# Scattering expert outputs by rank with plain writes, and finishing the last expert's slots on their own, in a mixture-of-experts decoder step

## What is computed

```python
# h = rmsnorm(x, ln_moe_g); 320 tokens, 4 groups of 8 experts, top-1 group, top-2 experts in it
hid = silu(xblk @ w_gate[e]) * (xblk @ w_up[e])          # per expert: (2048 x 512) twice
yb  = hid @ w_down[e]                                      # per expert: (512 x 2048)
y   = zeros(N + 1, D).at[slot_tok].add(yb * slot_w[:, None])
x   = x + y[:N]                                            # residual
out = rmsnorm(x, final_norm_g)                             # y_prompt (256 rows), y_sample (64 rows)
```

## Time and profile before

| | us |
|---|---|
| Median of 3 runs (1901.27 to 1910.1) | 1905.28 |
| The profiled execution's own time | 1904.04 |
| Its span, first to last instruction | 1902.2 |

### The profile page before, as it was taken

How to read it: one execution, slowest core, us unless ns; L and a number is a source line. 1 busy time by engine, 2 the same in 40 slices (tenths; PEclk the granted TensorE clock), 3 DMA queues, 4 the chain that set the end, 5 groups by cost and what they waited for, 6 DMA issues and landing times. The chain is left out here.

```text
span 1902.2 us, 35921 instructions
## 1 busy us (share of the span) xinstructions
PE 1783.8 (94%) x15586; PEld 1231.8 (65%) x15586; DVE 708.2 (37%) x1332; ACT 470.7 (25%) x787; POOL 110.2 (6%) x116
## 2 busy tenths in 40 slices
PE   7999998997979999998999999999999999999995
PEld 6999998875667799786555545455554444554542
DVE  4437777445558443764411211111111111111122
ACT  5446653341223322732211110111100000000001
POOL 0000003300101000001000000000000000000000
PEclk9999999898999999999999999999999999999998
DMA  8544550213535672648899999999999999999997
GB/s 252 153 127 118 140 130 15 69 36 129 170 116 224 212 206 81 199 135 320 350 414 423 426 422 423 426 422 421 421 422 426 421 420 421 415 423 425 421 426 272
DMA packets 191061, 545.60 MB, mean 287 GB/s; under 512 B 39432, under 2 KB 147400, under 8 KB 163172
## 3 DMA queue, kind: packets, MB, share of 16 engines
q1 hardware_dynamic: 183796, 517.51, 70.6%
q0 software_dynamic: 6768, 26.09, 4.4%
q10 hardware_dynamic: 392, 0.45, 0.1%
HBM read 524.47 MB, written 28.19 MB: 291 GB/s over the span
## 5 line engine op out<-in xcount | busy, mean ns | idle before, releaser
L2970 PE MATMUL p_u<-w_expert,xgT 128*64 128x256 f32 x2048 | 236.1, 384 | 26.3 <-DMA w_expert<-in_w_up_dram 26.3
L2970 PE MATMUL p_g<-w_expert,xgT 128*64 128x256 f32 x2048 | 232.0, 379 | 0.0
L2986 PE MATMUL p_y<-w_expert,hidT 128*64 128x512 f32 x960 | 217.8, 595 | 1.0 <-DMA w_expert<-in_w_down_dram 0.5
L2970 PEld LDWEIGHTS p_u<-w_expert,xgT 128*64 128x64 f32 x2048 | 146.9, 138 | 107.2 <-DMA w_expert<-in_w_up_dram 33.5
L2970 PEld LDWEIGHTS p_g<-w_expert,xgT 128*64 128x64 f32 x2048 | 146.5, 137 | 87.9 <-issue 18.1
L2937 PE MATMUL p_xg<-low,slot_sel 128*64 128x512 f32 x768 | 177.1, 596 | 0.0
L2986 PEld LDWEIGHTS p_y<-w_expert,hidT 128*64 128x64 f32 x960 | 66.1, 137 | 126.4 <-issue 124.2
L3092 DVE CAST row<-rowf 128x1 int32<-128x1 f32 x32 | 4.9, 154 | 362.7 <-POOLq L3273 354.5
L3086 DVE TENSOR_TENSOR xgT<-p_xgT,moe_gain 128x512 f32<-128x512 f32 x64 | 41.2, 686 | 202.0 <-PE p_xgT L2952 202.0
L2937 PEld LDWEIGHTS p_xg<-low,slot_sel 128*64 128x64 f32 x768 | 52.3, 137 | 79.5 <-issue 73.4
L3270 POOL DMA_INDIRECT x_dram<-y_slots,row x31 | 48.5, 1564 | 869.9 <-DVE y_slots L3103 869.9
(11 more groups left out here) (613 smaller groups left out, 2447.8 us busy)
## 6 DMA issues: line engine op xcount, KB each, us to landing
w_expert<-in_w_gate_dram SPq DMA_DIRECT2D x64, 2048.0 KB, 21.4
w_expert<-in_w_up_dram SPq DMA_DIRECT2D x64, 2048.0 KB, 23.2
w_expert<-in_w_down_dram SPq DMA_DIRECT2D x60, 2048.0 KB, 20.1
w_in_raw<-in_w_in_dram SPq DMA_DIRECT2D x32, 1024.0 KB, 5.8
ho_raw<-in_w_out_dram SPq DMA_DIRECT2D x12, 1024.0 KB, 7.1
q_lat<-in_w_out_dram SPq DMA_DIRECT2D x4, 1024.0 KB, 8.0
mem_k_s<-in_cache_mem_k_dram SPq DMA_DIRECT2D x8, 512.0 KB, 7.1
mem_v_s<-in_cache_mem_v_dram SPq DMA_DIRECT2D x8, 512.0 KB, 11.9
```

The costliest lines, as they stand in the source:

```text
L2970: mm = pe.matmul(acc[SL * h:SL * h + SL, 0:FF // 2], xgT[:, t, g // 2, :], w[g][:, FF * t + FF // 2 * h:FF * t + FF // 2 * h + FF // 2], s ...
L2986: mm = pe.matmul(p_y[SL * h:SL * h + SL, 512 * b:512 * b + 512], hidT[:, j, g, :], tile, start=(g == 0 and j == 0), stop=(g == 1 and j == 1))
```

## The change

Five edits. (1) `scatter` writes plainly instead of adding. The row index now has the rank in it: rank 0 rows go to the first 320 rows of a new DRAM tensor `rank_dram` (640 rows of 8 KB), rank 1 rows to the last 320. It is cleared in the recurrent-head stage by ten DMAs from a block of zeros. (2) The residual stays in SBUF (`h3`); the three DMAs that parked it in DRAM and the wait on them go. (3) For expert 1, `w[0]` is loaded in four pieces and `w[1]` in two, each as soon as TensorE has used that piece of expert 0. (4) SyncE, before it waits for the last uses, issues in order: two 4 KB gain rows, the sample rows of the residual (SBUF to SBUF, 512 KB), the last expert's granules (`w[5]` in halves), and, once the scatter of expert 30 has landed, both ranks' rows of all tokens (5 MB). The gain is spread over partitions by four matmuls. (5) The last expert's slots are not spread over the tokens. Their rows are handled as a fourth tile `slot_x`: x from the gathered `xg`, plus the other rank's row fetched by an indirect DMA, plus `p_y`; it is normed on its own and written over the outputs by two indirect DMAs on GpSimd, after the plain stores of the other tiles. The three other tiles are x + rank 0 + rank 1.

```diff
+                for i in range(4 * T // 128):
+                    sp.dma_start(S.rank_dram.rearrange("t (h n) -> (t h) n", h=2)[128 * i:128 * i + 128, :], zeros).then_inc(ranks_cleared, 16)
                 for j in range(HP):
...
+                sp.wait_ge(ranks_cleared, 16 * (4 * T // 128))
...
-        halves = S.x2_dram.rearrange("t (h n) -> (t h) n", h=2)
...
+        halves = S.rank_dram.rearrange("t (h n) -> (t h) n", h=2); w_part = sem("w_part_used"); w_early = sem("w_early_in")
...
+        total = S.final_a + [slot_x]; squares = S.final_b + [xgT[:, :, :, :].rearrange("p t h s -> p (t h s)")]
...
+                    if isinstance(r, int):
+                        for k in range(4):
+                            sp.wait_ge(w_part, k + 1)
+                            sp.dma_start(w[0][:, 1024 * k:1024 * k + 1024], w_granule(d, 0, 1)[:, 1024 * k:1024 * k + 1024]).then_inc(w_in[0] if k == 3 else w_early, 16)
+                        for k in range(2):
+                            sp.wait_ge(w_part, 5 + k)
+                            sp.dma_start(w[1][:, 2048 * k:2048 * k + 2048], w_granule(d, 1, 1)[:, 2048 * k:2048 * k + 2048]).then_inc(w_in[1] if k == 1 else w_early, 16)
+                        for g in range(2, 6):
+                            load(g, 1, r)
+                        first = 2
...
-                    with sp.Fori(first, NE) as e:
+                    with sp.Fori(first, NE - 1) as e:
                         for g in range(6):
                             load(g, e, r)
-                    for g in range(4):
-                        sp.wait_ge(w_free[g], NE * r + NE)
...
-                for i, n in enumerate(TILE):
-                    sp.dma_start(S.x2_dram[128 * i:128 * i + n, :], S.h3[0:n, i, :]).then_inc(S.parked, 16)
...
+                def finish(last):
                     sp.wait_ge(w_free[5], NE * last + STILLS[-1] + 1)
-                    sp.wait_ge(y_kept, 1)
-                    for i in range(2):
-                        sp.dma_start(S.final_x[i], S.x2_dram[128 * i:128 * i + 128, :]).then_inc(S.final_in[i], 16)
                     for h in range(2):
-                        sp.dma_start(S.final_x[2][64 * h:64 * h + 64, :], S.x2_dram[SEQ:T, D // 2 * h:D // 2 * h + D // 2]).then_inc(S.final_in[2], 16)
-                    sp.dma_start(S.final_g, d['final_norm_g'].unsqueeze(0).to_broadcast([128, D])).then_inc(S.final_g_in, 16)
+                        sp.dma_start(g_rows[64 * h:64 * h + 1, :], d['final_norm_g'].unsqueeze(0)[:, D // 2 * h:D // 2 * h + D // 2]).then_inc(g_in, 16)
+                        sp.dma_start(sample_x[64 * h:64 * h + 64, :], S.h3[0:64, 2, D // 2 * h:D // 2 * h + D // 2]).then_inc(S.final_in[2], 16)
+                    for g in range(5):
+                        load(g, NE - 1, last)
+                    sp.wait_ge(w_free[5], NE * last + NE - 1)
+                    sp.dma_start(w[5][:, 0:2048], w_granule(d, 5, NE - 1)[:, 0:2048]).then_inc(w_early, 16)
+                    sp.dma_start(w[5][:, 2048:4096], w_granule(d, 5, NE - 1)[:, 2048:4096]).then_inc(w_in[5], 16)
+                    sp.wait_ge(y_out, 16 * (NE * last + NE - 1))
+                    sp.dma_start(total[0], S.rank_dram[0:128, :]).then_inc(S.final_in[0], 16)
+                    sp.wait_ge(g_spread, 1)
+                    sp.dma_start(S.final_b[0], S.rank_dram[T:T + 128, :]).then_inc(S.final_in[0], 16)
+                    for k in range(2):
+                        for h in range(2):
+                            sp.dma_start((total, S.final_b)[k][2][64 * h:64 * h + 64, :], S.rank_dram[T * k + SEQ:T * k + T, D // 2 * h:D // 2 * h + D // 2]).then_inc(S.final_in[2], 16)
+                    sp.dma_start(total[1], S.rank_dram[128:256, :]).then_inc(S.final_in[1], 16)
+                    sp.dma_start(S.final_b[1], S.rank_dram[T + 128:T + 256, :]).then_inc(S.final_in[3], 16)
+                    sp.wait_ge(ready, 1)
+                    sp.dma_start(outs[0][0, 0:128, :], total[0]).then_inc(stored[0], 16)
+                    sp.wait_ge(ready, 2)
                     for h in range(2):
-                        sp.dma_start(S.final_g_halves[64 * h:64 * h + 64, :], d['final_norm_g'][D // 2 * h:D // 2 * h + D // 2].unsqueeze(0).to_broadcast([64, D // 2])).then_inc(S.final_g_in, 16)
-                    for i in range(2):
-                        sp.wait_ge(ready, i + 1)
-                        sp.dma_start(outs[0][0, 128 * i:128 * i + 128, :], out[i]).then_inc(stored, 16)
+                        sp.dma_start(outs[1].rearrange("b t n -> (b t) n")[:, D // 2 * h:D // 2 * h + D // 2], total[2][64 * h:64 * h + 64, :]).then_inc(stored[1], 16)
                     sp.wait_ge(ready, 3)
-                    sp.dma_start(outs[1].rearrange("b t n -> (b t) n")[:, 0:D // 2], out[2][0:64, :]).then_inc(stored, 16)
-                    sp.wait_ge(stored, 64)
-
-                rounds(sp, body, end)
+                    sp.dma_start(outs[0][0, 128:256, :], total[1]).then_inc(stored[0], 16)
+                    for kind in range(2):
+                        sp.wait_ge(stored[kind], 32)
+                    sp.wait_ge(slots_stored, 32)
+
+                rounds(sp, body, last_plain, finish)
...
+                            if parts and (g, t) in ((0, 1), (0, 3), (0, 5), (1, 3)):
+                                mm.then_inc(w_part, 1)
                         mm.then_inc(w_free[g], 1)
-
-                def down(g, r, e, skipped):
+                        if parts and g < 2:
+                            pe.wait_ge(w_free[g], 1)
+                            pe.nop().then_inc(w_part, 1)
...
+                    elif halved:
+                        pe.wait_ge(w_early, 80)
...
                     for j in range(2):
+                        if halved and j == 1:
+                            pe.wait_ge(w_in[4 + g], 16 * (RING * r + e - skipped + 1))
...
+                    if isinstance(r, int):
+                        expert(0, 0, True)
+                        pe.wait_ge(w_early, 64)
...
+                    n = NE * last + NE
+                    pe.wait_ge(g_in, 32)
+                    pe.wait_ge(found, 1)
+                    pe.wait_ge(xgT_v, 2 * n)
+                    for h in range(2):
                         for b in range(2):
-                            for h in range(2):
-                                hh = slice(SL * h, SL * h + SL)
-                                pe.matmul(into[i][2 * b + h][:, :], selT[hh, i, :], y[hh, 512 * b:512 * b + 512], start=True, stop=True).then_inc(scattered, 1)
-                    for b in range(2):
-                        pe.wait_ge(last_added, 1 + b)
+                            mm = pe.matmul((p_xg, p_xgT)[h][:, 512 * b:512 * b + 512], sel[64 * h:64 * h + 1, 0, :], g_rows[64 * h:64 * h + 1, 512 * b:512 * b + 512], start=True, stop=True)
+                    mm.then_inc(g_spread, 1)
+                    up(n)
+                    pe.wait_ge(g_kept, 2)
+                    turn_hidden(n)
+                    pe.wait_ge(hidT_done, n)
+                    pe.wait_ge(y_v, n - 1)
+                    pe.wait_ge(y_a, n - 1)
+                    down(0, last, NE - 1, len(STILLS))
...
+                    down(1, last, NE - 1, len(STILLS), True)
+                    add_pairs(2)
+                    add_pairs(3)
...
+                def find_places():
+
+                    def step(n, ins):
+                        ins.then_inc(found, 1)
...
+                def scale(i, gain):
+
+                    invert(i)
+                    dve.wait_ge(inverted, ORDER.index(i) + 1)
+                    dve.scalar_tensor_tensor(total[i], total[i], ss[:, i, 2:3], gain, ALU.mult, ALU.mult).then_inc(ready, 1)
...
+                def finish(last):
+                    n = NE * last + NE
+                    dve.wait_ge(row_sum, 3 * n)
+                    dve.memset(sel[:, 0, :], 1.0).then_inc(found, 1)
+                    find_places()
+                    dve.wait_ge(g_spread, 1)
+                    dve.tensor_copy(g_full[:, 0:1024], p_xg[:, :]).then_inc(g_kept, 1)
+                    dve.wait_ge(g_kept, 2)
+                    for h in range(2):
+                        dve.tensor_copy(g_fold[64 * h:64 * h + 64, :], g_full[64 * h:64 * h + 64, D // 2 * h:D // 2 * h + D // 2]).then_inc(g_kept, 1)
+                    hidden(n)
+                    copy_hidT(n)
+                    dve.wait_ge(S.final_in[0], 32)
+                    add(1, total[0], S.h3[:, 0, :])
+                    dve.tensor_tensor(total[0], total[0], S.final_b[0], ALU.add).then_inc(summed, 1)
+                    dve.wait_ge(slots_in, 16)
+                    add(2, slot_x.rearrange("p (q t) -> p q t", t=8), xg[:, :, :].rearrange("p t q -> p q t"))
+                    scale(0, g_full)
+                    dve.wait_ge(S.final_in[1], 16)
+                    add(3, total[1], S.h3[:, 1, :])
+                    dve.wait_ge(g_kept, 4)
+                    scale(2, g_fold)
+                    dve.wait_ge(S.final_in[3], 16)
```

(59 more changed lines are left out.)

154 lines of the change are left out of this document (71 added, 83 removed).

## The result

| | before | after |
|---|---|---|
| Median of 5 runs each, same chip | 1905.28 | 1924.43 (1918.89 to 1929.43) |
| Profiled execution, time | 1904.04 | 1919.13 |
| Its span | 1902.2 | 1917.4 |

The ratio is 1.0106, 95% interval 1.008 to 1.0132: slower by 1.1%, above my range of 1892 to 1912.

A forecast was written before the change was run, and what follows sets the result against it. DMA time bounds the expert stage, TensorE's slack being some 27 us. Last down weights 16.2 us earlier and a tail 12.7 us longer sum to -3.5: 1900.5 profiled, 1901.8 on the median; range 1892 to 1912.

The forecast's parts named there:

- Part 3, ten clears: Recurrent-head stage: clears cost nothing where DMA tenths are 0 to 2; bound 0 to 4 us if they delay state stores.
- Part 2, no parking, pieces: Front of the expert stage: dropping parked rows and loading weights in pieces gains 3.5 us, bounds 0 and 7.4.
- Part 3, new DMAs ahead of L: End of the expert stage: sample and gain rows ahead of the last weights delay them 1.3 us, bounds 1.2 and 2.6.
- L: The time the last down weights land, 1874.4 in the kernel before; predicted to move by -16 us.
- Part 1, plain scatters: Expert stage, scatters' queue: 31 plain scatters take 13 us in place of 27.4, 14 saved; bounds 15.4 and 0.
- Part 4, tile 0's rows after L: Tail: the first prompt tile's rows of both ranks are in 5.3 us after the last down weights land.
- Part 4, VectorE's chain: Tail: VectorE's sums, norms and scalings in code order, from 5.3 to 31.9 us after the last weights, plus 2 for GpSimd.
- Part 4, from the last scaling to the end: End of the tail: two indirect stores of 1.56 us issued one after the other, then 5 us for the last landing.
- the third rival (TensorE caps the gain): Expert stage: TensorE's 27 us of slack lie in 16 waits, so half of the 16 is lost: 1910; chance 0.08.
- the second rival: Expert stage, scatters' queue: a plain 4 KB row costs as much as an added one, saving nothing: 1916; chance 0.10.
- the signs that I had named for being wrong: Profile: software queue still at 3%; last down weights earlier by under 8; tail ending with the loads; TensorE without waits.
- The rival that ended slower: The rival headed "Slower", scatters' queue in the expert stage: plain rows as dear as added ones, 1916; chance 0.10.

The follow-up runs named there:

- run 1: The kernel before with only the ten clearing DMAs added, at the change's place in the recurrent-head stage; ratio 1.0045 to the kernel before.
- run 2: The changed kernel with its ten clears moved to an idle stretch in the output projection; ratio 1.0046 to the kernel before.
- run 4: The changed kernel with its 31 scatters adding into the rank rows instead of writing plainly; ratio 1.0180 to the kernel before.
- run 7: The changed kernel with expert 1's first two weights loaded whole instead of in six pieces; ratio 1.0080 to the kernel before.
- run 6: The changed kernel with only half the samples' residual copied, in the router stage, and nothing copied ahead of the last weights; ratio 1.0050 to the kernel before.
- run 8: The changed kernel with the samples' rank rows loaded over 128 partitions instead of 64 (samples' output not the reference's); ratio 1.0057 to the kernel before.
- run 9: The changed kernel with the samples' two sums on VectorE instead of GpSimd; ratio 1.0073 to the kernel before.

## Why the prediction was wrong, by its own steps

My sum for the profiled execution was 1900.5; it took 1919.13, 18.6 us more. The steps give the same within rounding:

| Step | predicted | measured | by |
|---|---|---|---|
| Part 3, ten clears | 0 | +7.0 | U; runs 1, 2 |
| Part 2, no parking, pieces | -3.5 | 0 | run 4 to the first still; run 7 |
| Part 3, new DMAs ahead of L | +1.3 | +7.1 | runs 4, 6 |
| Part 1, plain scatters | -14 | -15.4 | run 4 |
| Part 4, tile 0's rows after L | 5.3 | 9.1 | after; run 8 |
| Part 4, VectorE's chain | 28.6 | 28.8 | after |
| Part 4, from the last scaling to the end | 6.6 | 6.5 | after |

**The failing step is Part 3's "nobody waits for these until the stage ends".** I asked who waits for the transfers behind the clears, and had the DMA tenths as proof of an empty queue. I did not ask what else uses the engines without being a DMA of the program: TensorE's instructions do, and TensorE waited 4.9 us for them. My bound of 4 us was too low, too, as it was made from the state stores.

**The second is a price by bytes.** I priced 0.5 MB of sample rows at 2.35 us/MB, the rate of rows over 128 partitions, and again in the 5.2 MB of the tail. Removing one such copy gave back 4 us, not 1.3; spreading the other moved the rows from L + 9.0 to L + 5.3 and from L + 18.4 to L + 12.9, which are the 5.3 and 13 of the prediction. Of the 7.1 us ahead of L, some 3 stay open: the gain rows and the rank loads queued at 1858, of which I isolated none. They may not be there at all. The 7.1 and the 15.4 of Part 1 come out of the same subtraction, and 15.4 is 2.6 more than the scatters' prices give; with 12.8 for Part 1 only half a microsecond is left over.

**Part 2** read the front rightly up to the first down weights: they landed 32.9 us after U for 34.7. But by the next granule the lead was 0.2 us, and the kernels with the same scatters are level at the first still expert. TensorE was 99% busy from 960 to 1100 us, and the next load can't be issued before it has used the buffer, so earlier weights waited for it: what the third rival (TensorE caps the gain) says, at another place than the one where I looked.

**Part 1** was right, in place and size, and so refutes the second rival: a plain row cost half of an added one. **Part 4** was right in mechanism; its start was late by the price above, and two of its sizes are right by luck. The exchange between VectorE and GpSimd, for which I took 2 us, cost VectorE 3.3 (3.55 + 4.42 for 2.35 + 2.29) and GpSimd 4.1 (3.98 + 4.27 for twice 2.08). That is nearer to 4.2 each than to my 2; to move the sums to VectorE gained 1.6 net (run 9). The exclusive lock that the Trainium skill states ("SBUF — State Buffer", section "SBUF: two separate sides") gives 4.2, so the trace agrees with it better than with my halving. The operations bear it out one by one. In the changed kernel VectorE's sum for the slots' tile ends at 1888.69. Behind it GpSimd's first sum, VectorE's scale, GpSimd's second sum and VectorE's next sum end at 1890.90, 1893.04, 1895.24 and 1897.39: each ends 2.1 or 2.2 us after the one on the other engine, which is about what it takes alone.

The chain is 28.8 for 28.6 all the same, because the three norms took 2.7, 2.6 and 2.4 us for 3.0, 3.0 and 2.6. And the last step is 6.5 for 6.6 by three misses: from the last scaling to the second indirect store's issue it was 2.1 us for 1.56, the store landed 2.6 us after its issue where I took 5 (the 2.5 that the prediction gives beside it was nearer), and 1.7 us from that landing to the end of the span were not in my sum.

Of the signs that I had named for being wrong, one came: L was earlier by 1.3 us, where I had put the limit at 8. TensorE's waits were 16.0 us and not 11.

The rival that ended slower was the wrong one. The outcome lies on its side of the forecast by two costs that no rival named.

## What to carry to other kernels

Before placing a large transfer in a quiet stretch, look at the instruction queue as well as at the tenths: here a burst that filled the DMA engines was free beside long matmuls (37 in 5 us) and cost 7 us beside short ones (126 or more), whose instructions came over the same engines. Price a DMA by its shape, partitions first, and by a row of the same shape; half the partitions had 0.56 to 0.58 of the rate, and delayed what was queued ahead of it. When work is moved behind the end of the bound resource, its whole latency counts, stores and indirect stores too, and a saving of 15 us in the stream can be spent on a tail that is serial.

## What was not expected of the hardware

- Ten DMAs of 512 KB in a row idled TensorE for 4.9 us in waits that name no producer and that end 1.4 to 1.6 us after a packet of instructions; the same DMAs elsewhere idled it for none.
- A 64-partition DMA ran at 236 to 238 GB/s with the engines 1.02 to 1.03 busy, against 412 over 128 partitions.
- A plain indirect write took 2.8 us/MB, an adding one 5.3.
- A DMA whose source order is half, then row, moved about 52 GB/s at a share of 0.13, and the load issued behind it held SyncE's queue for 10.49 us.
- Twelve matmuls of the gather took 2.93 us with four of them over 64 rows, and 2.78 with all over 128: the smaller contraction was no faster, and the change of shape cost about 0.1 us.
- VectorE and GpSimd, both summing tiles in SBUF, did not share the time but took turns, operation by operation.
